# Three terms of the gate and up products accumulated in one PSUM range of an expert layer

## The reference, cut to what matters

```python
def expert(args):
    ids, wg, wu, wd = args
    xg = xt[ids]
    return (jax.nn.silu(xg @ wg) * (xg @ wu)) @ wd

ye = lax.map(expert, (idx, w_gate, w_up, w_down))
ye = ye * gate[..., None].astype(ye.dtype)
```

## Time and profile before

| | |
|---|---|
| median of 3 runs | 2787.26 us (2785.95 to 2791.68) |
| span of the profiled execution | 2782.5 us |
| its own time less its span, taken as median less span | 4.8 us |
| TensorE matmul records, busy | 2568.6 us, 92% of the span |
| TensorE weight loads, busy | 2363.0 us, 85% |
| VectorE busy | 1533.8 us, 55% |
| ScalarE busy | 1275.9 us, 46% |
| mean granted TensorE clock | 0.951 of 2.4 GHz |
| bytes by DMA | 624.39 MB |

### The profile page before, as it was taken

One profiled execution on the slowest core, in us unless ns is written; L12 is line 12 of the kernel. 1 busy time (PEld: TensorE's weight loads), 2 busy tenths in 40 slices (PEclk: granted clock), 3 DMA queues, 4 the chain that ended last, 5 costly groups with the idle time before them and its releaser, 6 DMA issues.

```text
span 2782.5 us, 52629 instructions
## 1 busy us (share of the span) xinstructions
PE 2568.6 (92%) x21830; PEld 2363.0 (85%) x21830; DVE 1533.8 (55%) x2167; ACT 1275.9 (46%) x1979; POOL 296.5 (11%) x174
## 2 busy tenths in 40 slices
PE   7999978989797499999999999999999999999997
PEld 5777867857576499999999999999999999999997
DVE  4610138848833566565655656556565565565663
ACT  6311225744422245555545555454545455455453
POOL 3221111111220101011010110101101011010100
PEclk9999987978899699999999999999999999999998
DMA  3122110020234499998999989999899999998994
GB/s 114 50 77 74 60 33 1 1 62 1 99 113 167 149 317 331 308 330 289 332 298 310 333 285 335 295 305 330 289 337 299 304 319 300 339 302 298 323 338 130
DMA packets 447726, 624.39 MB, mean 224 GB/s; under 512 B 15669, under 2 KB 380309, under 8 KB 447509
## 3 DMA queue, kind: packets, MB, share of 16 engines
q1 hardware_dynamic: 439844, 602.79, 64.7%
q0 software_dynamic: 7664, 18.25, 3.2%
HBM read 597.23 MB, written 23.69 MB: 223 GB/s over the span
## 4 chain that ended last, share of the span: by engine, by line
PE 48%; issue 5%; DVE 5%; DMA 5%; ACT 3%; POOL 0%; SPq 0%; POOLq 0%; ACTq 0%; DVEq 0%
PE ps L1719 20%; PE ps L1735 16%; PE ps L1723 10%; DVE wlo L1845 4%; DMA wgu<-in_w_up 4%; ACT whi L1785 2%; PE ps L1747 1%; PE ps L1708 1%; ACT xx L1792 1%; ACT xb L1793 1%; ACT sil L1821 0%; DMA xg<-xn_rows,take 0%; DMA out_rows<-yr,give 0%; ACT low L1810 0%; DVE vals L1853 0%
## 5 line engine op out<-in xcount | busy, mean ns | idle before, releaser
L1719 PE MATMUL ps<-xx,whi 128*128 128x264 f32 x5632 | 793.0, 295 | 67.4 <-issue 62.6
L1845 DVE TENSOR_TENSOR wlo<-wgu,whi 128x2048 bf16<-128x2048 f32 x352 | 804.4, 2285 | 22.7 <-ACT whi L1785 22.7
L1719 PEld LDWEIGHTS ps<-xx,whi 128*128 128x128 f32 x5632 | 727.5, 194 | 73.4 <-issue 65.3
L1735 PE MATMUL ps<-hid,wd 128*128 128x132 f32 x5632 | 708.0, 279 | 0.3
L1785 ACT ACTIVATE whi<-wgu 128x2048 fp32r<-128x2048 f32 x352 | 669.8, 1903 | 4.1 <-DMA wgu<-in_w_up 4.1
L1735 PEld LDWEIGHTS ps<-hid,wd 128*128 128x128 f32 x5632 | 660.2, 190 | 2.3 <-DVE hid L1895 0.8
L1810 ACT ACTIVATE low<-ps 128x264 f32<-128x264 f32 x352 | 137.5, 391 | 876.9 <-PE ps L1723 876.9
L1723 PE MATMUL ps<-xb,wlo 128*128 128x132 bf16 x5632 | 397.9, 223 | 0.0
L1895 DVE TENSOR_TENSOR hid<-sil,gu 128x132 f32<-128x132 f32 x352 | 104.5, 297 | 519.0 <-ACT sil L1821 513.0
L1723 PEld LDWEIGHTS ps<-xb,wlo 128*128 128x128 bf16 x5632 | 335.1, 98 | 17.2
L1893 DVE TENSOR_TENSOR gu<-ps,low 128x264 f32<-128x264 f32 x352 | 152.1, 432 | 198.0 <-ACT low L1810 197.9
(11 more groups left out here) (222 smaller groups left out, 2346.5 us busy)
## 6 DMA issues: line engine op xcount, KB each, us to landing
wgu<-in_w_gate SPq DMA_DIRECT2D x176, 1024.0 KB, 6.9
wgu<-in_w_up SPq DMA_DIRECT2D x176, 1024.0 KB, 9.5
wd<-in_w_down SPq DMA_DIRECT2D x176, 1024.0 KB, 10.9
w<-in_w_in SPq DMA_DIRECT2D x28, 512.0 KB, 4.9
zv_rows<-qn SPq DMA_DIRECT2D x24, 256.0 KB, 2.0
wo<-in_w_out SPq DMA_DIRECT2D x8, 512.0 KB, 7.7
out_rows<-x SPq DMA_DIRECT2D x8, 512.0 KB, 2.9
xn_rows<-xn SPq DMA_DIRECT2D x8, 512.0 KB, 2.6
```

The costliest lines, as they stand in the source:

```text
L1719: pe.matmul(banks(b + i)[:, 0:2 * C2], whi[m % 2][:, i, k], xx[:, k], start=(k == 0), stop=False, skip_group_check=True)
L1735: mm = pe.matmul(y_tile(k), wdown[j % ND][:, c, k * P:(k + 1) * P], hid[m % 2][:], start=(m == 0 and k % PER_BANK == 0), stop=(m == M - 1) ...
L1845: nc.vector.tensor_tensor(wlo[m % 2][:], wgu[gu_slot(j)][:, :, :, c * P:(c + 1) * P], whi[m % 2][:].bitcast(F32), ALU.subtract).then_inc(l ...
```

## The change

The high part and the rest of the rows are no longer sent through TensorE as one run of 264 columns. For each of the 16 tiles of `whi` there are two matmuls, one by the 132 columns of the high part and one by the 132 columns of the rest, and both add into the same 132 PSUM columns; the `wlo` term adds there too. Gate and up take two halves of one bank, so a step has one bank and not two. The copy `low` and the sum `gu` go, with their tiles and semaphores: silu reads the gate half from PSUM, and the multiplication reads the up half from PSUM. `up` now waits for `whi` at its start and for `wlo` only ahead of the third term, and `hid_ready` of two steps before takes the place of `sum_ready`. On ScalarE silu moves ahead of the split of weights in every step, and has a wait for `hid` of two steps before; the multiplication on VectorE has a wait for `down` of two steps before.

```diff
 def up(ex, m, first):
-    pe.wait_ge(lo_ready, M * ex + m + 1)
+    pe.wait_ge(hi_ready, M * ex + m + 1)
     if not (first and m < 2):
-        pe.wait_ge(sum_ready, M * ex + m - 1)
-    b = 2 * (m % 2)
+        pe.wait_ge(hid_ready, M * ex + m - 1)
+    sums = [banks(m % 2)[:, C2 * i:C2 * (i + 1)] for i in range(2)]
     for i in range(2):
         for k in range(KD):
-            pe.matmul(banks(b + i)[:, 0:2 * C2], whi[m % 2][:, i, k], xx[:, k], start=(k == 0), stop=False,
-                      skip_group_check=True)
+            for part in (0, C2):
+                pe.matmul(sums[i], whi[m % 2][:, i, k], xx[:, k, part:part + C2], start=(i == k == part == 0),
+                          stop=False, skip_group_check=True)
+    pe.wait_ge(lo_ready, M * ex + m + 1)
     for i in range(2):
         for k in range(KD):
-            mm = pe.matmul(banks(b + i)[:, 0:C2], wlo[m % 2][:, i, k], xb[:, k], start=False, stop=(k == KD - 1),
+            mm = pe.matmul(sums[i], wlo[m % 2][:, i, k], xb[:, k], start=False, stop=(k == KD - 1),
                            skip_group_check=True)
     mm.then_inc(gu_done, 1)
...
 # ScalarE, body
-        src = banks(b)[:, 0:1024].rearrange("p (i n) -> p i n", i=2)
-        nc.scalar.activation(low[m % 2][:], src[:, :, C2:2 * C2], ACT.Copy).then_inc(low_ready, 1)
+        if not (first and m < 2):
+            act.wait_ge(hid_ready, n - 2)
+        nc.scalar.activation(sil[m % 2][:], banks(m % 2)[:, 0:C2], ACT.Silu).then_inc(sil_ready, 1)
+        if m == M - 1 and not last:
+            split_rows(ex + 1, False)
         then = ahead(ex, m, last)
-        if m == M - 1:
-            act.wait_ge(sum_ready, n)
-            nc.scalar.activation(sil[m % 2][:], gu[m % 2][:, 0], ACT.Silu).then_inc(sil_ready, 1)
-            if not last:
-                split_rows(ex + 1, False)
         if then:
             split_high(*then)
-        if m < M - 1:
-            act.wait_ge(sum_ready, n)
-            nc.scalar.activation(sil[m % 2][:], gu[m % 2][:, 0], ACT.Silu).then_inc(sil_ready, 1)
...
 # VectorE, body
-        dve.wait_ge(low_ready, n)
-        src = banks(b)[:, 0:1024].rearrange("p (i n) -> p i n", i=2)
-        nc.vector.tensor_tensor(gu[m % 2][:], src[:, :, 0:C2], low[m % 2][:], ALU.add).then_inc(sum_ready, 1)
         dve.wait_ge(sil_ready, n)
-        nc.vector.tensor_tensor(hid[m % 2][:], sil[m % 2][:], gu[m % 2][:, 1], ALU.mult).then_inc(hid_ready, 1)
+        if not (first and m < 2):
+            dve.wait_ge(d_done, n - 2)
+        nc.vector.tensor_tensor(hid[m % 2][:], sil[m % 2][:], banks(m % 2)[:, C2:2 * C2], ALU.mult).then_inc(hid_ready, 1)
```

More of the change, by code:

```diff
@@ L1576, in experts @@
     xb = tiles("xb", [P, KD, C2], BF16)
-    low = [tiles(f"low{i}", [P, 2, C2]) for i in range(2)]
-    gu = [tiles(f"gu{i}", [P, 2, C2]) for i in range(2)]
     sil = [tiles(f"sil{i}", [P, C2]) for i in range(2)]
@@ L1595, in experts @@
         sem(s) for s in "take_ready xg_loaded xgT_done xgT_ready xh_ready xb_ready xl_ready".split())
-    hi_ready, lo_ready, gu_done, low_ready, sum_ready, sil_ready, hid_ready, d_done = (
-        sem(s) for s in "hi_ready lo_ready gu_done low_ready sum_ready sil_ready hid_ready d_done".split())
+    hi_ready, lo_ready, gu_done, sil_ready, hid_ready, d_done = (
+        sem(s) for s in "hi_ready lo_ready gu_done sil_ready hid_ready d_done".split())
     yT_ready, y_done, yr_ready = (sem(s) for s in "yT_ready yt_done yr_ready".split())
@@ L1806, in body @@
                     n = M * ex + m + 1
-                    b = 2 * (m % 2)
                     act.wait_ge(gu_done, n)
-                    src = banks(b)[:, 0:1024].rearrange("p (i n) -> p i n", i=2)
-                    nc.scalar.activation(low[m % 2][:], src[:, :, C2:2 * C2], ACT.Copy).then_inc(low_ready, 1)
-                    then = ahead(ex, m, last)
-                    if m == M - 1:
-                        act.wait_ge(sum_ready, n)
-                        nc.scalar.activation(sil[m % 2][:], gu[m % 2][:, 0], ACT.Silu).then_inc(sil_ready, 1)
-                        if not last:
-                            split_rows(ex + 1, False)
+                    if not (first and m < 2):
[3 more added lines that the diff above has]
+                        split_rows(ex + 1, False)
+                    then = ahead(ex, m, last)
                     if then:
                         split_high(*then)
-                    if m < M - 1:
-                        act.wait_ge(sum_ready, n)
-                        nc.scalar.activation(sil[m % 2][:], gu[m % 2][:, 0], ACT.Silu).then_inc(sil_ready, 1)
                     if m in OUT_STEPS and not first:
```

## The result

The changed kernel takes 3408.25 us (median of 4 runs, 3406.01 to 3410.29); the kernel before 2787.66 us (4 runs, 2785.95 to 2791.68). The ratio is 1.2226 with a 95% interval of 1.2211 to 1.2241: 621 us more, where I forecast 551 and a range up to 3455.

A forecast was written before the change was run, and what follows sets the result against it. TensorE was taken to bound the kernel inside an expert, with transfers keeping up. 2782.5 us of span + 555 for slower matmuls - 4 for the `wlo` wait = 3333, and 4.8 to the median: 3338 us, range 3265 to 3455.

The forecast's parts named there:

- the three pieces of a step: TensorE's matmuls of lines 1719, 1723 and 1735: 2.03, 0.95 and 1.76 us, alone setting the 4.74 us step.
- The one open price: Cost of a float32r matmul by 132 columns with its own load: taken as 113 ns, the load as bound, chance 0.80.
- the 107 of my load lengths: Weight-path time of 128 four-byte columns, from loads of 94 and 188 ns; as pace the lower bound, +491 us.
- The 113 of line 1735: Pace in ns of loads of the same form and length as `whi`'s on that line; taken for the new matmuls.
- The sum: 32 matmuls take 3.61 us in place of 2.03: +1.58 us a step, x 352 = +555 us, less 4 for `wlo`.
- the 13 waits: TensorE's "issue" waits at the edge of the loop over experts, 62.6 us in total, expected to stay.
- 20 us more at most: Upper-bound allowance for slow loads after each loop edge: some 1.5 us more, 13 times.
- the likeliest case: The load sets the pace of the new matmuls at 113 ns: 3338 us, bounds 3265 to 3455, chance 0.80.
- Signs that I had named: Trace signs: 11264 matmuls and as many loads 113 ns apart, 6.3 us steps, DMA share 0.74, 13 edge waits remaining.
- the second rival: Float32r is slow on few columns: 0.22 us for each new matmul, +1764 us, 4547 us; chance 0.06.
- The covered parts: `low` and `gu` (0.39, 0.43 us a step), silu and multiplication lie under TensorE's 4.74 us: worth nothing to the step.

The follow-up runs named there:

- the half-load one: Changed kernel with the 16 matmuls by the rest of the rows loading 64 columns of `whi` in place of 128: 3087.09 us (one run).
- the bf16 one: Changed kernel with `whi` and `xx` as bf16 tiles, a coarser split, same count of instructions: 2806.25 us, ratio to before 1.0078.
- the moved kernel: Changed kernel with 16 transposes into an unused bank (32 instructions) ahead of TensorE's first expert: 3336.54 us, ratio 1.1984.
- the moved bf16 kernel: Changed kernel with `whi` and `xx` in bf16, plus 16 transposes ahead of TensorE's first expert: 2743.08 us, ratio to before 0.9847.

## Why the prediction was right, and where it was short

**What bounds the kernel.** TensorE, by the three pieces of a step: right. The step grew by the piece that changed and by nothing else that the rows show.

**The price of a matmul.** The one open price was chosen among 60, 107, 113 and 121 ns, by the row of the nearest load. It is 112. That the load sets it was an argument before; the experiments show it: halving the load takes 0.05 us off a pair, halving the columns takes nothing, bf16 loads bring the pace to 58 ns. The Trainium skill, TensorE: Matmul & The Clock Gate, section "LDWEIGHTS (loading the stationary operand)", gives a load as its columns over 1.2, in ns, 107 for 128 columns. For four-byte weights the trace agrees within 5%: 112 from load to load, and 51 ns less length for 64 columns fewer.

That I took 113 and not the 107 of my load lengths was luck. The 113 of line 1735 need not be a pace of loads: the kernel before has plain float32 records with loads of only 16 columns, on line 1418, and they cost as much a column.

```profile
808.77 1.92 PE L1418 MATMUL ps<-xnT,wr 128*16 128x128 f32 x16
```

These start (1.92 - 0.27) / 15 = 110 ns apart for 128 columns, so 132 would take 113 with hardly any load. That makes a rival which I had not set out: float32r by few columns at the price of one such record, 0.22 us halved, the same 112 ns and the same total. The result cannot tell it from mine. The experiments do: it would have left the half loads at 112 ns and brought the 66 columns near 57, and neither was so.

**The sum.** 352 steps by +1.58 us give 555; the step shown has the 3.61 us that this counts with.

**The term that was mis-sized** is the one on the loop's edge. I left the 13 waits as they were and gave the half clock after them 20 us more at most, counted for one `up` an edge. Measured, there were 26 waits, 75.7 us and not 62.6. The half clock lasted through the second `up` into `down` at 7 of the 13 edges; in all TensorE worked 168 us at half clock behind the edges, before 64. The 32 matmuls take 7.07 us there and not 3.61, so about half of the added 104 us, 52, is lost. And the first expert, which begins at half clock, took 148.9 us where 107.9 + 22 x 1.58 = 142.7 was due. 13 + 52 + 6 = 71 us: these are the 70 between 3338 and 3408.

The second stall comes, by all that the runs show, from where the loop's first instructions lie: it stood after exactly 6 matmuls in the changed kernel, in the half-load one and in the bf16 one, whatever their pace, and 32 instructions ahead of the loop removed it twice. So it is an accident of the changed code's length and no price of the three terms. That the moved kernel hits 3338 within 2 us is luck: its stalls are 37 us shorter than I kept (25.6 in all and not 62.6), and its half clock costs some 45 us more than in the kernel before (154 us of work against 64), of which the likeliest case had nothing.

**The half clock.** In the changed kernel and in the moved one the clock rose at every edge behind 16 bf16 matmuls: by the eighth matmul of the second `up`, or within the first 6 records of `down`. With only 66 columns in every second matmul it fell also inside experts, and in the moved bf16 kernel it was back some 5.5 us after the stall's end. No experiment varied one of these things alone, so what made the stretches longer stays open.

**Signs that I had named.** As many loads as matmuls and the pace: as said. The DMA share came to 0.70 and not 0.74, since an expert took 156 us and not 149. The 13 waits became 26, and a granted clock of 0.5 inside an expert, named as a cost that I don't count, is what most of the 70 us are. One sign was badly chosen: for the second rival I had asked for records much longer than 230 ns that are over 200 ns apart. They are 275 ns long and still 112 apart, so the length of a record told nothing here.

**The covered parts.** `low`, `gu` and the order on ScalarE and VectorE were priced at nothing, and nothing of them shows in the step.

## What to carry to other kernels

Before a matmul is cut into narrower ones, count its weight loads: a piece whose columns stream faster than its tile loads pays for the load, and for four-byte weights of 128 columns that was 112 ns here, not far from the 127 ns of a whole matmul by 264 columns. If the pieces must be narrow, bf16 weights restore the pace (58 ns), at the price of a coarser split. And when a change alters the length of a loop's body, look at the loop's edge in the new trace before putting the whole difference down to the change: here some 50 of 621 us, and in bf16 the sign, hung on where 32 instructions put the loop.

## What the hardware showed that I had not expected

- At the edge of the loop TensorE stands still, and goes on 2.2 to 3.4 us after a 16 KB packet of instructions has begun to come (251 such packets in the changed kernel, 4.11 MB). In the changed code, before the 32 instructions moved it, it stood still twice: 2.6 to 4.5 us more each time with float32r, 4.8 to 5.4 us in bf16.
- The first stall was 1.7 to 2.3 us in the changed kernel, 2.6 to 3.1 with half the loads, 4.3 to 4.7 with bf16, at the same place in the code, and 4.7 to 4.9 in the kernel before. Why the slower matmuls shorten it was not tested.
- 16 transposes in a wait of TensorE, ahead of the first expert, made that expert 8.5 us faster: it began at full clock and not at half.
- Fewer columns made a kernel slower: 66 in place of 132 in every second matmul cost 46 us in one run, by the clock, at the same pace of loads.
